# Two feed-forward layers in float32 on one core: which output columns go through seven half-size products, and which engine makes their low parts

## The reference, cut to what matters

```python
# first layer
hf = rmsnorm(x, norm_ffn_g)
x = x + (silu(hf @ w_gate) * (hf @ w_up)) @ w_down      # w_gate, w_up: 1024 x 2816
...
# second layer
h = rms_norm(x, norm_ffn_pre)
f = (silu(h @ w_ffn_gate) * (h @ w_ffn_up)) @ w_ffn_down
x = x + rms_norm(f, norm_ffn_post)
```

## Time and profile before

| | us |
|---|---|
| median of 3 runs (1930.59 to 1931.03) | 1930.87 |
| the profiled execution, its own time | 1931.03 |
| its span, first to last instruction | 1929.2 |
| TensorE busy | 1909.5 (99%) |
| VectorE busy | 1255.4 (65%) |
| ScalarE busy | 731.5 (38%) |
| GpSimd busy | 251.6 (13%) |

### The profile page before, as it was taken

The page is one execution under the profiler, slowest core; times in us unless marked ns, Lnnn a source line. Parts: engine busy times, 40 slices in busy tenths (PEclk is TensorE's granted clock), DMA queues, the critical chain, the costliest instruction groups (busy, mean ns, idle before and its releaser), DMA issues.

```text
span 1929.2 us, 26476 instructions
## 1 busy us (share of the span) xinstructions
PE 1909.5 (99%) x10664; PEld 1603.2 (83%) x10664; DVE 1255.4 (65%) x1916; ACT 731.5 (38%) x1255; POOL 251.6 (13%) x155
## 2 busy tenths in 40 slices
PE   9999999999999999999999999999999999999998
PEld 7788888888888888999987778877777877999987
DVE  7777543344455747778765766757777567878765
ACT  6322322233333444444435522234444344444432
POOL 1121210011111113000004001111100132100002
PEclk9999999999999999999999999999999999999999
DMA  5222233332321333233333222221121422233322
GB/s 183 90 77 88 82 88 116 90 96 66 91 63 49 116 92 97 96 108 101 99 96 115 79 76 78 91 85 56 57 65 39 126 66 87 88 118 102 107 85 83
DMA packets 54562, 172.85 MB, mean 90 GB/s; under 512 B 6027, under 2 KB 11603, under 8 KB 54440
## 3 DMA queue, kind: packets, MB, share of 16 engines
q1 hardware_dynamic: 53056, 169.93, 28.4%
q10 hardware_dynamic: 1384, 1.22, 0.2%
HBM read 168.91 MB, written 2.22 MB: 89 GB/s over the span
## 4 chain that ended last, share of the span: by engine, by line
PE 89%; DVE 6%; ACT 3%; issue 1%; POOL 1%; DMA 0%; SPq 0%; DVEq 0%; ACTq 0%; POOLq 0%
PE PS L1472 21%; PE PS L1474 21%; PE PS L1473 21%; PE PS L1512 5%; PE PS L1514 5%; PE PS L1513 5%; DVE WL L2270 1%; PE PS L1841 1%; PE PS L1863 1%; PE PS L1639 1%; PE PS L1654 1%; PE PS L1819 1%; PE PS L1700 1%; PE PS L1686 1%; PE PS L1677 1%
## 5 line engine op out<-in xcount | busy, mean ns | idle before, releaser
L1472 PE MATMUL PS<-HH,WH 128*128 128x512 f32 x1132 | 447.7, 396 | 3.6 <-DVE WL L2270 2.7
L1474 PE MATMUL PS<-HH,WL 128*128 128x512 f32 x1132 | 441.2, 390 | 0.0
L1473 PE MATMUL PS<-HL,WH 128*128 128x512 f32 x1132 | 440.6, 389 | 0.0
L1910 ACT ACTIVATE WH<-RAW 128x1024 fp32r<-128x1024 f32 (+2 forms) x266 | 268.3, 1009 | 359.4 <-PE PS L1474 298.0
L2270 DVE TENSOR_TENSOR WL<-RAW,WH 128x1024 fp32r<-128x1024 f32 (+2 forms) x209 | 255.9, 1225 | 130.7 <-ACT WH L1910 127.4
L1472 PE MATMUL PS<-AH,WH 128*128 128x512 f32 x856 | 338.8, 396 | 1.4 <-DVE WL L2270 0.9
L1474 PE MATMUL PS<-AH,WL 128*128 128x512 f32 x856 | 333.7, 390 | 0.0
L1473 PE MATMUL PS<-AL,WH 128*128 128x512 f32 x856 | 333.2, 389 | 0.0
L1472 PEld LDWEIGHTS PS<-HH,WH 128*128 128x128 f32 x1132 | 212.5, 188 | 52.6 <-issue 6.7
L1474 PEld LDWEIGHTS PS<-HH,WL 128*128 128x128 f32 x1132 | 212.5, 188 | 45.3
L1473 PEld LDWEIGHTS PS<-HL,WH 128*128 128x128 f32 x1132 | 212.7, 188 | 42.7 <-issue 0.5
(11 more groups left out here) (308 smaller groups left out, 2194.7 us busy)
## 6 DMA issues: line engine op xcount, KB each, us to landing
RAW<-wst SPq DMA_DIRECT2D x290, 512.0 KB, 3.6
RAW<-wst SPq DMA_DIRECT2D x24, 256.0 KB, 2.6
RAW<-wst SPq DMA_DIRECT2D x8, 384.0 KB, 3.1
XT<-xT SPq DMA_DIRECT2D x3, 512.0 KB, 7.4
AR<-mx SPq DMA_DIRECT2D x4, 256.0 KB, 5.8
AR<-scr SPq DMA_DIRECT2D x16, 64.0 KB, 4.3
AR<-scr SPq DMA_DIRECT2D x8, 128.0 KB, 4.8
AR<-w SPq DMA_DIRECT2D x2, 512.0 KB, 3.9
```

Of the source, the lines that this page charges most:

```text
L1472: T.matmul(out, wh, XH[:, k, :], start=k == 0, stop=False)
L1473: T.matmul(out, wh, XL[:, k, :], start=False, stop=False)
L1474: m = T.matmul(out, wl, XH[:, k, :], start=False, stop=k == nk - 1)
L1910: t = A.activation(whole(WH, i, n), raw(i)[:, 0:n], ACT.Copy, scale=1.0)
```

## The change

Three things are edited. The second layer is no longer paired: PAIRED goes from both layers to the first only, so its 14 pairs (gate2 and up2, j = 8 to 21) become 28 units, its down2 units are no longer put between pairs, and its forms are gone. In the first layer PAIR_FROM goes from 8 to 6, so gate 6, 7 and up 6, 7 become two more pairs, and the pairs gate 6, up 6 and gate 8 follow each other with no down unit in between. In the first layer's pairs the low parts of chunks 1, 2, 5 and 6 are made by POOL; and forms_x and forms become one item, so a round of the forms takes three steps in place of four.

```diff
-PAIRED = ("", "2")
-PAIR_FROM = 8
+PAIRED = ("",)
+PAIR_FROM = 6
...
-LO_ON_POOL = ()
+LO_ON_POOL = (1, 2, 5, 6)
...
-    forms = [(f, m) for m in range(4) for f in (e.forms_x, e.forms, e.forms_hi, e.forms_lo)]
+    forms = [x for m in range(4) for x in ((e.forms, m), (e.forms_hi, m), (e.forms_lo, m))]
...
-            def forms_x(s, sfx, m):
-                g = "fpre2" if sfx else "ffn_g"
+            def forms(s, sfx, m):
+                g, b22 = "fpre2" if sfx else "ffn_g", VT[:, 0:256]
+                T0, T1, T2, T3, T4, T5, T6 = (TF[:, 256 * n:256 * n + 256] for n in range(7))
...
                 t = scaled(TF[:, 512:1024], m + 4, 0, 512)
                 t.then_inc(*dve_done["ffn"].next("forms", "x", sfx, m))
-
-            def forms(s, sfx, m):
-
-
-                T0, T1, T2, T3, T4, T5, T6 = (TF[:, 256 * n:256 * n + 256] for n in range(7))
                 dve.wait_ge(*at("forms", "x", sfx, m))
```

More of the change, by code:

```diff
@@ L297 @@
     pair_products = pair_keep = pair_held = pair_add = pair_silu = pair_hi = pair_lo = none
-    chunk_add = chunk_hi = chunk_lo = forms_x = forms = forms_hi = forms_lo = none
+    chunk_add = chunk_hi = chunk_lo = forms = forms_hi = forms_lo = none
     last_products = last_evict = last_fold = last_factor = last_norm = last_add = last_out = none
@@ L2314, in scaled @@
                                                   op0=ALU.mult, op1=ALU.mult)
-                scaled(TF[:, 0:256], m, 0, 256)
+                scaled(T0, m, 0, 256)
                 scaled(VT[:, 0:256], m, 256, 512)
```

## The result

| | before | changed |
|---|---|---|
| median of the timed runs, us | 1930.73 (1929.77 to 1931.03) | 1953.68 (1950.70 to 1955.82) |
| the profiled execution, its own time | 1931.03 | 1949.94 |
| its span | 1929.2 | 1947.9 |

The ratio is 1.0112, 95% interval 1.0100 to 1.0125. The change costs 23 us by the medians of the table and 19 us in the profiled execution. The changed kernel's median is of four executions that lie in two pairs, 1950.7 and 1951.7, 1955.6 and 1955.8; over all 18 executions of it on record the median is 1951.7 (1949.94 to 1955.82), to which the ratio is nearer. The forecast was 1942.8 in a range of 1939.5 to 1947. The direction is as forecast, the time is not, and two kinds of loss have to be found: 7 us in the profiled execution, and another 2 (18 executions) to 4 (the four of the table) between it and the median.

A forecast was written before the change was run, and what follows sets the result against it. TensorE, busy 99% of the span, was taken as the bound. The terms 13.2 - 2.0 - 2.3 + 2.1 + 0.9 = +11.9 us on 1930.87 gave about 1942.8, range 1939.5 to 1947.

The forecast's parts named there:

- +13.2: Second layer unpaired: 41 units at 5.44 us, 223.0 against 209.8, so +13.2 us with nothing hiding it.
- -2.0: First layer, two more pairs: four units become two pairs, -2.0 us.
- the -2.3 of the second layer's waits: Second layer: TensorE's two waits for weights' low parts behind the forms can't occur without forms, -2.3 us.
- The forms' rounds: First layer, three-step rounds: VectorE's lag makes TensorE wait, about +2.1 us, between 0 and 5.
- The walk: Queues followed through the first layer's forms rounds: waits of 1.1 to 1.2, 0.3 and about 0.6 us.
- The row of three pairs: First layer, no down unit between: bank slack 0.6 and -0.1 us, two boundaries cost 0.9 together, between 0 and 4.
- Low parts on GpSimd at no cost between down units: First layer's pairs: low parts come 0.7 us later, up to 1.4 more if blocked, yet cost 0.
- Some 3.5 us in hand: First layer's pairs: chunks 2 and 3 done at 856.05, product 2 due at 859.6.
- Rival B: GpSimd's low parts delay each of 16 pairs by 0.7 us, about 1952; decides from a 30.75 us period; chance 0.12.
- A: Rival: first layer hides the forms' lag and the row runs smoothly, +8.9, 1939.8 us; chance 0.15.
- C: Rival: unpaired matmuls run faster in the relieved second layer, returning 13 us, 1930; chance 0.03.
- the two waiting terms: First-layer waits from the three-step forms (+2.1, up to 5 us) and the three pairs in a row (0.9, up to 4).

The follow-up runs named there:

- e1: Kernel before with only the second layer unpaired; 1941.55 us (ratio 1.0058).
- f3: e2 with an empty item behind each round of the forms, so a round has four steps again while the merged item stays; 1941.66 us (1.0061).
- e4: Changed kernel with the forms' scaled copies and sums as two items again, 16 items for 18 steps; 1953.03 us (1.0117).
- g1: Changed kernel with a fourth raw buffer for one unit, up 7; 1950.47 us (1.0102).
- g2: g1 with all low parts of chunks on VectorE; 1945.24 us (1.0078).
- h3: Changed kernel profiled again, nothing altered; 1951.68 us.
- e2: Changed kernel with PAIR_FROM back at 8, so no two pairs stand side by side; 1945.58 us (1.0080).
- h1: Changed kernel run and profiled again, nothing altered; median 1952.73 us (1.0117), profiled execution 1953.63.
- h2: Changed kernel profiled again, nothing altered; 1954.24 us.
- f2: Kernel before with only the low parts of chunks 1, 2, 5 and 6 moved to GpSimd, in all 28 pairs; 1933.25 us (1.0011).
- f1: Kernel before, both layers paired, with one step in five left free of forms in the second layer; 1928.55 us (0.9993).

## Why the prediction was right or wrong

**The matmul counts: right.** +13.2 and -2.0, and the -2.3 of the second layer's waits: e1 gave 1941.55 for an expected 1941.7, and in the changed kernel the pairs are 9.90 and the units 5.44 us. The waits behind the forms and in the row are where the text put them.

**The forms' rounds: the term was mis-sized, and a step in it failed.** The walk gave 1.5 us for the two waits ahead of the pairs and 0.6 at the first chunks; the trace has 4.4 and 1.5. Apart from GpSimd's low part (2.9 us, as it was in the earlier trace rows) the walk used each instruction's undisturbed duration, though the text had shown that an instruction of VectorE with two SBUF inputs is held up by one of GpSimd. Three cases of the two engines holding each other up (0.36 us on GpSimd at 725, 0.95 and 1.1 on VectorE at 739.5 and 746) put 2.4 us into the walk; a fourth, 0.56 on VectorE at 726, was covered by a wait. The Trainium skill, SBUF — State Buffer, "Who interferes with whom", has the rule that an instruction of VectorE with two SBUF inputs contends with one of GpSimd that reads SBUF, and the trace agrees with it again: the low part of 0.69 us that began at 746.15 beside a GpSimd instruction running from 745.53 to 747.39 ended 0.55 after it. The prediction applied the rule to throughput, where it mattered little, and not to the latency of a chain in which both engines take turns. f3, and e4 with it, show that the cadence is the cause and merging is not. How much of the excess over the walk is interference is read from durations in one trace; no run took it away alone.

**The row of three pairs: mis-sized, 0.9 forecast, 3.8 measured.** The step said that the slack of the PSUM bank was 0.6 and -0.1 us and that delays on VectorE show. It looked for delays in work and left out the raw buffers: with three of them, a pair behind a pair can load its second block only when the pair before has made its low parts, and VectorE's weight sum stands in the queue in front of the addition that frees the bank. g1 and g2 show it: the excess falls from 5.9 to 3.7 and from 7.8 to 2.7. What the raw buffer leaves of the row's loss in g1, 1.9 us, falls to 0.9 in g2, with the low parts on VectorE.

**Low parts on GpSimd at no cost between down units: right in the first profile, in f3 and in h3, wrong in others.** 0.6 us in e2, 1.6 in e4, 2.5 and 3.2 in h1 and h2, and 3.0 in the median of f2 with 28 such pairs. "Some 3.5 us in hand" was read at one place of a period in a kernel in which GpSimd was idle. The period's busy times were sized too low as well: 12.5 us on GpSimd and 21.7 on VectorE in the window of 30.75, for 10 to 11 and 19 to 20. They add up to 34.2, more than the 30.75 from which B was to decide, and TensorE has no hole in it, so that sum isn't the test. Rival B, with 11 us in all pairs, had the right mechanism and three to four times the size; its time, 1952, is near the result for the most part by the other two terms, and that is no confirmation.

**A, C and the range.** A is refuted by the first wait, C by e1 and by the rate of 226.7 ns. The range ended at 1947 because the bounds of the two waiting terms, 5 and 4 us, were noted and then not added: 1930.87 + 8.9 + 5 + 4 = 1948.8. The first bound was itself too low, 5 against the 5.9 measured (4.4 ahead of the pairs and 1.5 at the first chunks). Even 1948.8 and the 3.2 us of B's mechanism that h2 shows, 1952.0, would take in the median of the 18 executions and not the 1953.68.

**Open.** The profiled executions of g1 and g2, 1948.93 and 1946.22, differ by 2.7 us. That the rest of the 5.2 us between their medians is late low parts in steady pairs is argued from h1 and h2, not shown: neither has any there. No profile is of one of the slowest executions, 1955.6 and 1955.8. Why the late low parts come in some executions and not in others was not found, nor why the granted clock holds through the last matmuls in four of the 16 profiles (15.4 to 15.5 us to the end) and falls in the others (16.4 to 16.8).

## What to carry to other kernels

Price a removed or added matmul by the distance between starts in the trace, 117.9 ns for 256 columns against 226.7 for 512 here, and check a stage's total by it: that part of this forecast was right to 0.2 us. When a wait is forecast from a chain across queues, walk it with the durations that instructions have beside each other, not with the undisturbed ones, and follow every buffer on the way, the loads' too; where two pieces of work are put next to each other that used to have something light between them, look first at the buffers that were enough for the lighter order. Add the upper bounds of all waiting terms before the range is written. And before terms are summed against one profiled execution, see whether its untouched parts, the end of the program above all, took what they took before.

## What the runs showed of the hardware that was not expected

At a single wait of 2.7 us on TensorE, with TensorE busy up to it, the granted clock fell to 1.2 GHz in three of four profiles of the changed kernel, and in six of nine of all kernels here that have this wait; 512-column matmuls then started every 0.43 us, in the changed kernel for 3.4 us in two profiles and 6.8 in the third. VectorE kept its durations in that stretch (1.21 us for a low part of 128x1024 in h2 at 747.5 as in the first profile at 747.9), and in the two the loss was caught up, since TensorE was ahead of its weights. In the second layer's mixers, at the same instructions in h3 (near 1075 us) and f1 (near 1068), a stretch of 3.4 us cost 1.6.
